# Outer products of a retention state, contracted over 64 partitions in place of 128, in a one-core decoder step

## The reference

```python
def retention_chunk(S, q, k, v, log_gamma):      # here L = 1
    ...
    k_dec = k * jnp.exp((L - 1.0 - i)[:, None] * log_gamma[None, :])[None, :, :, None]
    S_new = jnp.exp(L * log_gamma)[None, :, None, None] * S + jnp.einsum('blhd,blhe->bhde', k_dec, v)
    return S_new, intra + cross
```

## Time and profile before

| what | value |
|---|---|
| median of the runs | 2592.5 us |
| the profiled execution, its own time | 2592.5 us |
| its span on the core | 2590.8 us |
| granted TensorE clock, mean over the span | 0.982 of full |
| TensorE busy | 2480.5 us, 96% |
| VectorE busy | 1192.9 us, 46% |
| ScalarE busy | 993.3 us, 38% |
| GpSimd busy | 125.6 us, 5% |

### The profile page before, as it was taken

How to read it: one execution, slowest core, us unless ns; L and a number is a source line. 1 busy time by engine, 2 the same in 40 slices (tenths; PEclk the granted TensorE clock), 3 DMA queues, 4 the chain that set the end, 5 groups by cost and what they waited for, 6 DMA issues and landing times.

```text
span 2590.8 us, 43830 instructions
## 1 busy us (share of the span) xinstructions
PE 2480.5 (96%) x18904; PEld 2242.3 (87%) x18904; DVE 1192.9 (46%) x1648; ACT 993.3 (38%) x1376; POOL 125.6 (5%) x268
## 2 busy tenths in 40 slices
PE   5999999999979999999999999999999999999997
PEld 4999999965578999889899999887777999999997
DVE  3433235644456433236633325755555646633235
ACT  4322235526455322235522224633223546422233
POOL 0000000112200000000000000002222100000000
PEclk9999999999989999999999999999999999999999
DMA  6555235793544655475565435454545445543244
GB/s 254 172 155 155 72 127 173 256 230 113 163 130 139 195 149 156 141 241 166 155 187 155 119 103 176 153 176 163 170 164 171 135 147 163 164 131 97 76 151 145
DMA packets 116867, 407.14 MB, mean 157 GB/s; under 512 B 23099, under 2 KB 23227, under 8 KB 116291
## 3 DMA queue, kind: packets, MB, share of 16 engines
q1 hardware_dynamic: 81154, 282.65, 34.9%
q10 hardware_dynamic: 19584, 69.21, 8.6%
q0 software_dynamic: 15936, 52.47, 6.2%
HBM read 380.87 MB, written 23.41 MB: 156 GB/s over the span
## 4 chain that ended last, share of the span: by engine, by line
PE 83%; DVE 8%; ACT 5%; issue 2%; DMA 2%; SPq 0%; ACTq 0%; POOL 0%; POOLq 0%; DVEq 0%
PE PS L1733 66%; PE PS L1187 3%; DVE WL L1953 3%; PE PS L1693 3%; ACT WH L1813 2%; PE PS L1140 1%; PE PS L1751 1%; ACT Y L1857 1%; PE PS L613 1%; PE PS L1094 1%; PE PS L1125 1%; PE PS L1135 1%; DVE X L2020 1%; PE PS L1106 1%; PE PS L545 1%
## 5 line engine op out<-in xcount | busy, mean ns | idle before, releaser
L1953 DVE TENSOR_TENSOR WL<-RAW,WH 128x1024 fp32r<-128x1024 f32 (+1 forms) x468 | 617.6, 1320 | 805.0 <-ACT WH L1813 804.0
L1733 PE MATMUL PS<-HH,WH 128*128 128x260 f32 x3584 | 839.0, 289 | 51.1 <-DVE HL L2040 37.5
L1733 PE MATMUL PS<-HH,WL 128*128 128x260 f32 x3584 | 818.8, 284 | 0.0
L1733 PE MATMUL PS<-HL,WH 128*128 128x260 f32 x3520 | 802.6, 284 | 0.0
L1813 ACT ACTIVATE WH<-RAW 128x1024 fp32r<-128x1024 f32 (+1 forms) x468 | 528.6, 1130 | 425.6 <-PE PS L1733 309.6
L1733 PEld LDWEIGHTS PS<-HH,WH 128*128 128x128 f32 x3584 | 596.6, 190 | 104.0 <-issue 86.3
L1733 PEld LDWEIGHTS PS<-HH,WL 128*128 128x128 f32 x3584 | 597.1, 190 | 0.0
L1733 PEld LDWEIGHTS PS<-HL,WH 128*128 128x128 f32 x3520 | 585.2, 190 | 0.8 <-issue 0.2
L1733 PE MATMUL PS<-GH,WH 128*128 128x260 f32 x1408 | 376.8, 288 | 12.3 <-DVE WL L1953 12.3
L1733 PE MATMUL PS<-GL,WH 128*128 128x260 f32 x1408 | 372.2, 285 | 0.0
L1733 PE MATMUL PS<-GH,WL 128*128 128x260 f32 x1408 | 371.8, 285 | 0.0
(11 more groups left out here) (291 smaller groups left out, 2234.5 us busy)
## 6 DMA issues: line engine op xcount, KB each, us to landing
RAW<-in_w_in SPq DMA_DIRECT2D x224, 512.0 KB, 3.6
RAW<-in_w_out SPq DMA_DIRECT2D x112, 704.0 KB, 4.2
AW<-in_w_ada ACTq DMA_DIRECT2D x128, 512.0 KB, 3.6
RAW<-in_w_odd SPq DMA_DIRECT2D x60, 512.0 KB, 3.6
RAW<-in_w_even SPq DMA_DIRECT2D x28, 512.0 KB, 4.4
RAW<-in_w_odout SPq DMA_DIRECT2D x28, 512.0 KB, 3.6
AFIRST<-in_w_ada SPq DMA_DIRECT2D x4, 2048.0 KB, 19.8
RAW<-in_w_evout SPq DMA_DIRECT2D x16, 512.0 KB, 3.8
```

What stands on the lines that cost most here:

```text
L1733: last = nc.tensor.matmul(ps[:, x, 0:HT], w[:, at_ + k * P:at_ + (k + 1) * P], src[k0 + k][:, x, :], start=(begin and t == 0), stop=(end a ...
L1953: nc.vector.tensor_tensor(WL[:, at_:at_ + w], RAW[:, from_:from_ + w], WH[:, at_:at_ + w].bitcast(F32), ALU.subtract).then_inc(lo_done, 1)
```

## The change

`outer` names only partitions 0 to 63 of both operands, and the two memsets of partitions 64 to 127 are dropped. Nothing reads these partitions any more. Number, place, output size, waits and signals of the 64 matmuls stay.

```diff
@@ outer(n), on TensorE
                 after(pe, st_new, n)
-                nc.tensor.matmul(PS[2][:, 1, :], KMB[:, b % 4, d * P:(d + 1) * P], VX[:],
+                nc.tensor.matmul(PS[2][:, 1, :], KMB[0:2 * CGS, b % 4, d * P:(d + 1) * P], VX[0:2 * CGS, :],
                                  start=True, stop=True).then_inc(outer_done, 1)
@@ odd_dve, step 12 of stage odin, on VectorE
                 if i == AHEAD["odin"]:
                     pack_samples()
-                    nc.vector.memset(KMB[2 * CGS:P].bitcast(F32), 0.0)
-                    nc.vector.memset(VX[2 * CGS:P, :].bitcast(F32), 0.0)
```

## The result

The changed kernel takes 2613.28 us (median of 6 runs, 2610.0 to 2615.33) against 2593.84 us before (2590.18 to 2599.29), ratio 1.0070, 95% interval 1.0056 to 1.0085. The profiled execution took 2613.64 us, its span is 2612.0 us: 21.2 us more than the span of before. By the medians the growth is 19.4 us, and the interval allows 14.5 to 22.0. Lines of `products`, `WL` and the streamed blocks are two lower than before, L1094 to L1148 are the same.

The account below looks back on a forecast made before the run. TensorE was taken as the bound, busy 96% of the span and alone setting the pace in this stage. Switches 22.0, waits -1.4 and memsets 0 gave +20.6 us on 2592.5, so 2613.1 us, range 2602 to 2618.

Parts of the forecast that it names:

- The pace: Stage of the outers: TensorE alone sets the pace, busy 59.84 of 60 us, VectorE at about half.
- The streaming: The 64 outer matmuls keep 512 moving columns, so fewer rows gain nothing: value 0.
- The possible 1.0 us of gain: Streaming of the 64 fp32r outers: a small gain not excluded, at most 64 x 0.015 = 1.0 us.
- fp32r of 64 rows switches: At each outer: 64 rows switch the array's shape like line 545's fp32 matmuls, 0.39 us per full visit.
- Rivals 1 and 2: At the outers: 1, fp32r isn't switched, 2592.5 us, chance 0.10; 2, half of each switch is paid, 2603, chance 0.05.
- 113 switches: Around the 64 outers: 128 switches less 12 behind cross and 3 ahead of keys, 49 full visits and 15 halves.
- The term of 22.0 us: Cost of the new shape switches around the outers: 113 x 0.195 = 22.0 us.
- The waits: Three outers waiting for VectorE's update hide part of the delay: 0.9 + 0.5, 1.4 us back.
- Rival 3: Outers' lateness passes through update and `st_new`, so more outers wait: 2616.5 us, chance 0.05.
- The memsets: VectorE loses 0.91 + 0.48 us at 1688.68, hidden by a 7.10 us weight load: value 0, bounds 0 and -1.4.
- the forecast's case: Whole kernel: outers pay the full switch price, 2608 to 2617 us at 0.16 to 0.21 us per switch, chance 0.78.

Follow-up runs that it names:

- experiment 2: Kernel before with memsets kept, the matmul of outer contracting 96 partitions instead of 128: 2593.03 us, ratio 0.9998.
- experiment 3: Changed kernel with each 64-row outer issued twice in a row into the same bank: 2626.45 us, ratio 1.0133.
- experiment 4: Kernel before with memsets kept, only the 12 outers directly behind a cross contracting 64 partitions: 2591.60 us, ratio 1.0012.
- experiment 5: Kernel before with the two memsets moved from VectorE to GpSimd, outers kept at 128 partitions: 2591.03 us, ratio 0.9999.
- experiment 7: Kernel before with streamed adaLN blocks multiplied in pairs and the keys job padded from 64 to 128 output columns: 2576.55 us, ratio 0.9954.

## Why the prediction was right, step by step

**The pace.** That TensorE sets the pace in the stage held: its added 19.5 us between the first and the last outer arrive in full at the end. The last streamed block starts at 2335.1 us against 2314.3, 20.8 later; the first one, at 89.9 against 89.4, was already 0.5 late, from before anything that the change touches, and the first outer, at 1739.3 against 1738.5, 0.8.

**The streaming.** Value 0 held. 128 rows, 96 rows (experiment 2) and the second of two 64-row matmuls (0.22, experiment 3) step 0.22 to 0.23 us. The possible 1.0 us of gain isn't there.

**fp32r of 64 rows switches.** This was the open choice, made by the likeness to line 545. It held, in full: 0.39 to 0.40 us per visit. The rule of the Trainium skill (TensorEngine Tiling (Array Packing), Key Properties) that a change of tiling mode drains the engine fits; its other rule (TensorE: Matmul & The Clock Gate, Why this matters for your kernels), that a single matmul of small contraction takes as long as a full one, is right of the matmul (0.22 us in experiment 3) and misses the neighbourhood. Rivals 1 and 2 are out: the first by 20 us, the second since both halves of each switch show in the time line.

**113 switches.** The half visits behave as counted (experiment 4 and the rows behind a cross and ahead of keys). The term of 22.0 us is a little too large: where small transposes follow an outer (lines 1119 and 1148, 128 columns, 9 places by my count), less than 0.10 is added behind it. First before, then after:

```profile
1787.95 0.40 PE L1094 MATMUL PS<-VX,KMB 128*128 128x512 f32 x1
1788.19 0.60 PE L1119 MATMUL PS<-IDENT,KR 128*128 128x128 f32 x4
```

```profile
1792.22 0.50 PE L1094 MATMUL PS<-VX,KMB 64*128 64x512 f32 x1
1792.65 0.66 PE L1119 MATMUL PS<-IDENT,KR 128*128 128x128 f32 x4
```

The four records last 0.66 instead of 0.60 us. That is 0.06 more where longer matmuls get 0.10 to 0.11, so some 0.05 less at each place: 9 x 0.05 = 0.4 us less than the term has.

**The waits.** 1.4 us taken back was right in kind: TensorE's waits for VectorE vanish. In size and number two errors nearly cancel. From the outer at 1745.23 to the matmul behind the next one at 1749.52 are 4.29 us in the earlier trace rows; after, it is 4.48 (1746.86 to 1751.34, above). Two outers' own steps, one way in and one way out should have added 0.20 + 0.10 + 0.09 + 0.20 = 0.59, and 0.19 came: a wait gives back 0.40 us, not the 0.48 of the prediction (0.31 + 0.17). And there are four: the prediction held that TensorE has no other idle time in the stage, but an outer in the last head also started late without being listed as a wait. In the kernel before:

```profile
1980.25 3.59 PE L1135 MATMUL PS<-VR,KT 128*128 128x512 f32 x8
1983.97 0.47 PE L1094 MATMUL PS<-VX,KMB 128*128 128x512 f32 x1
```

Eight steps of 0.43 end at 1983.69, 0.28 us ahead of it. So 4 x 0.40 = 1.6 us come back, and the stage's growth is 22.0 - 1.6 - 0.4 = 20.0 us by the corrected terms. Measured: 322.6 - 303.1 = 19.5 between the first and the last start, plus 0.1 ahead of the first outer and 0.3 at and behind the last: 19.9. Rival 3, lateness passed on, is excluded by the view of waits, which lists none in the stage.

**The memsets.** Value 0 held, by a thin margin that the prediction doesn't give. TensorE's waits from 1683 to 1700 (for whom, us in total, times, longest) but for those on `HL`, 1.8 us in both, first before, then after:

```profile
PE PS L1733 <- DVE TR L1375: 0.8, 1, 0.8
PE PS L1172 <- DVE WL L1953: 0.3, 1, 0.3
```

```profile
PE PS L1731 <- DVE QRS L1385: 1.1, 1, 1.1
PE PS L1172 <- DVE WL L1951: 0.2, 1, 0.2
```

Before, TensorE does wait 0.8 us for the rotation, which stands behind the memsets, and 0.3 us more for the weights. Without the memsets the first wait is gone and the time is spent in the next two: 1.3 us of waits instead of 1.1, because the load still takes its time, 7.07 us from 1688.72 on the chain. So the load hides the memsets with 0.3 us to spare. How long it takes differs between executions. In that of experiment 2 the chain that ended last runs through the memsets and not through the load:

```profile
1687.39 0.91 DVE KMB L1587
...
1688.36 0.48 DVE VX L1588
```

There the two paths end nearly together: `WL` is ready at 1695.82 and line 1172 starts at 1695.91. So VectorE's memsets cost nothing here because a load of this length runs beside them, not because they are far from the path. In experiment 5, without them on VectorE, TensorE waits 1.7 us for `WL` at this place, beside a load of 7.37 us.

**The number.** That the forecast of 2613.1 lies within 0.2 us of the median is partly luck: the stage grew 0.7 less than forecast and the rest of the program, which varies by a few us between runs, happened to be 1.3 us longer. The forecast was also added to a median of 2592.5, where that of all six runs is 2593.84: against that, 20.6 was forecast and 19.4 measured. The range of the forecast's case, 2608 to 2617, doesn't quite follow from its own 0.16 to 0.21 us per switch, which gives 2609 to 2615.

## What to carry to other kernels

A matmul that uses fewer rows of the array isn't cheaper, and if its shape makes the array switch, its neighbours pay: here 0.2 us for each way in and out, on a queue that had no idle time. Zero rows that keep a matmul at full size are free; look for such matmuls between full-size ones, pad them, or put those of one shape side by side. Read the price from the distances between starts, since the busy share stays at 100% while less is done, and look whether the next weight load still starts ahead of its matmul.

## What the runs showed of the hardware that was not expected

- The number of rows doesn't matter as such: 96 rows behave like 128 (steps of 0.23 us), and 64 don't (0.43).
- A change of shape can be seen in the weight loads: the first load of the new shape starts with its matmul (both at 1758.89 after the change, and so at all 64 outers), where it started 0.03 to 0.24 us ahead at the 52 outers that had no switch before.
- fp32r matmuls of 32 and 64 output columns don't switch (0.23 to 0.24 us per step in the earlier trace rows), while fp32r ones of 64 rows (0.43 us) and fp32 ones of 64 columns (0.35 us around the keys job) do. Widening the latter to 128 columns removed it (experiment 7). Why fp32r differs by direction wasn't tried.
- The way out of a narrow shape is cheaper ahead of transposes of 128 columns (0.06 us on the group) than ahead of longer matmuls (0.10).
